# Four norm roots by reciprocal and square root, and the first weights' high parts moved to ScalarE, in a two-layer decoder step

## The chip, the cores and the metric

The kernel runs on one core of a Trainium2 chip. The metric is the device time of one execution in microseconds, the median of several runs.

## The reference

One inference step of a decoder trunk with two layers, for 512 prompt tokens and 8 x 4 sample tokens that share all weights, all in fp32. Width D is 1024. Each layer computes

```
h = rms_norm(x, gain) * (1 + scale) + shift      # shift, scale, gate g from silu(c) @ w_mod
x = x + g1 * mixer(h)                            # layer 0: forgetting attention and pooling; layer 1: native sparse attention
h = rms_norm(x, gain2) * (1 + scale2) + shift2
x = x + g2 * ((silu(h @ w_gate) * (h @ w_up)) @ w_down)

rms_norm(x, gain) = x * rsqrt(mean(x * x) + 1e-6) * gain
```

There are four norms over the model's width: before each mixer and before each SwiGLU. The mixers also norm their heads of 64; the diff does not touch these.

## The kernel before, in words

Activations lie feature by token: x is X, 8 chunks of 128 features by NT = 544 tokens (512 prompt, 32 sample), and the normed rows are H. Every large product is made of three products of parts: a matrix is split into a high part (a copy rounded to the fp32r type, WH or XH) and a low part (the value less the high part, WL or XL), and `product` (line 480) sums high x high, high x low and low x high, with 272 columns (HALF) each. The work is a sequence of stages; in each, every engine has its own program and they meet at semaphores. At the end of a stage all engines wait for each other. A `Chain` (`link`, line 77) makes an engine wait for its own last instruction.

**The norm.** ScalarE squares the chunks, VectorE sums them. TensorE multiplies the sum with a matrix of ones (`root_pe`, line 394), which gives the mean square of each token on all 128 partitions. VectorE makes V from it (line 402). ScalarE computes R = exp(-0.5 ln V) (`root_act`, lines 387 to 392) and VectorE refines R by one Newton step of three operations (`newton`, line 866). While ScalarE works, VectorE does what `root_dve` (line 399) is given as `meanwhile`. Then `norm_dve` (line 439) makes the 32 sample columns of H in three operations (lines 451 to 453), and the prompt columns chunk by chunk: H (line 462), on ScalarE XH with the shift added (`norm_act`, line 418), on VectorE XL (`low`, line 458). The H of chunk k + 1 stands before the XL of chunk k in VectorE's order. TensorE's first product of a stage waits for the weights' first cut and for the XL of chunk 0.

**The four places.** Norm 0 has its root in the setup stage (lines 237 and 305), with small index work (`small`) as `meanwhile`; the first input projection then takes the ready root. The norm before layer 1's mixer is in the input projection of `nsa_w_in`, called "in" like the first (`linear`, line 487, called at 3137). There `meanwhile` is `cut_first` (line 624): take the first half of the first 256 weight columns from RAW, cast it to WH (line 477) and subtract to WL (line 478), then let SP load the next block into that half. The norms before the SwiGLUs are in `swiglu` (line 701). Their `meanwhile` is `Seven.cut_eight` (line 969): two casts and two subtractions of 128 x 1024 (lines 972 and 973) for the first of 22 weight blocks; when they are done (`cut`, value 1) SP may load the third block into the same slot (`load`, line 912). The second block is cut by `high_eight` on ScalarE and `low_eight` on VectorE, between the first products.

**Other work around them.** In setup SP issues the loads of inputs and modulation weights, and in advance the raw weights of the first projection. In layer 0's SwiGLU TensorE also multiplies the modulation weights of layer 1 (`mod_bite`, line 330) ahead of its first product, as they land. In the two input projections side work runs between the weight blocks: the forget gate's log-sigmoid (`Forget`, ScalarE at lines 1181 to 1183: absolute value, exponential, logarithm; VectorE reads it at line 1201) and the gates of the sparse attention (`Gates`, exponential at line 1276, reciprocal at line 1287). ScalarE loads a table of functions (ACT_TABLE_LOAD) where a function isn't in the one that it holds.

Of the kernel before, what the change touches and what calls it, by code (L numbers as in the profile page):

```python
# [88 lines left out]
class Kernel:  # L89
# [297 lines left out]
    def root_act(self, act, n):  # L387
        nc, s = self.nc, n["sem"]
        act.wait_ge(s["v"], 1)
        nc.scalar.activation(n["R"], n["V"], ACT.Ln).then_inc(s["ln"], 1)  # L390
        act.wait_ge(s["ln"], 1)
        nc.scalar.activation(n["R"], n["R"], ACT.Exp, scale=-0.5).then_inc(s["r"], 1)
# [6 lines left out]
    def root_dve(self, dve, link, n, meanwhile):  # L399
        s, V = n["sem"], n["V"]  # L400
        dve.wait_ge(s["ms"], 1)
        link(self.nc.vector.tensor_scalar(V.rearrange("p (h n) -> p h n", h=2), self.ps[:, 0:2, 0:HALF], 1.0 / D, EPS, ALU.mult, ALU.add))
        dve.sem_inc(s["v"], 1)
        meanwhile()
        dve.wait_ge(s["r"], 1)
        newton(self.nc, link, n["R"], V, n["S"])

    def norm_act(self, act, n, XH, keep, meal=None, between={}):


        nc, H, s = self.nc, self.H, n["sem"]
        if n["V"] is not None:
            self.root_act(act, n)
        act.wait_ge(s["decode"], 1)
        nc.scalar.copy(XH[:, :, TP:NT], H[:, :, TP:NT]).then_inc(s["x_high"], 1)
        for k in range(KD):
            act.wait_ge(s["h"], k + 1)
            nc.scalar.activation(XH[:, k, 0:TP], H[:, k, 0:TP], ACT.Identity, bias=n["sh"][:, k, 0:1]).then_inc(s["x_high"], 1)
            if meal and k == 1 and meal[3] == KD:
                self.mod_rows(act, meal[0], meal[3] // KD - 1)  # L420
            if k in between:
                between[k]()
        for k in range(KD if keep else 0):
            act.wait_ge(s["x_cut"], k + 2)
            nc.scalar.activation(H[:, k, 0:TP], H[:, k, 0:TP], ACT.Identity, bias=n["sh"][:, k, 0:1]).then_inc(s["kept"], 1)
# [13 lines left out]
    def norm_dve(self, dve, link, n, XH, XL, cut_first, meal=None):  # L439
# [7 lines left out]
        if n["V"] is not None:  # L447
            self.root_dve(dve, link, n, cut_first)
        else:
            cut_first()  # L450
# [10 lines left out]
        for k in range(KD):  # L461
            nc.vector.scalar_tensor_tensor(H[:, k, 0:TP], X[:, k, 0:TP], A[:, k, 0:1], R[:, 0:TP], ALU.mult, ALU.mult).then_inc(s["h"], 1)
            if k == 0:
                dve.wait_ge(s["x_high"], 1)
                nc.vector.tensor_tensor(XL[:, :, TP:NT], H[:, :, TP:NT], XH[:, :, TP:NT].bitcast(F32), ALU.subtract).then_inc(s["x_cut"], 1)
            else:
                low(k - 1)
# [19 lines left out]
    def linear(self, name, w, K, blocks, x=None, out=None, residual=None, norm=None, first=None, meal=None, more=None, beside=None, squares=False, root=None, into=None, loaded=None):  # L487
# [8 lines left out]
        with self.stage() as (sb, sem):  # L496
# [12 lines left out]
            dc, x_high, x_cut, slices = sem("dc"), sem("x_high"), sem("x_cut"), sem("w_slices")  # L509
# [4 lines left out]
            with nc.Block() as block:  # L514
# [80 lines left out]
                def _(act):  # L595
                    for m in range(2):
                        act.sem_inc(pfree[m], 1)
                    if norm:
                        self.norm_act(act, n_, XH, True, meal)
# [16 lines left out]
                def _(dve):  # L616
# [7 lines left out]
                    def cut_first():  # L624
# [13 lines left out]
                        if not first:  # L638
                            dve.sem_inc(free[0], 1)

# [48 lines left out]
                    if norm:  # L689
                        self.norm_dve(dve, link, n_, XH, XL, cut_first, meal)  # L690
# [10 lines left out]
    def swiglu(self, l, meal=None, more=None):  # L701
# [3 lines left out]
        with self.stage() as (_, sem_a):  # L705
            DOWN = H[:, :, :].rearrange("p k n -> p (k n)")[:, 0:KF // 2 * 256].rearrange("p (k n) -> p k n", k=KF // 2)
            down_in = sem_a("down_in")
            with self.stage() as (sb, sem):
# [10 lines left out]
                with nc.Block() as block:  # L719
# [34 lines left out]
                    def _(act):  # L754
# [10 lines left out]
                        self.norm_act(act, n_, XH, True, meal, {2: lambda: seven.high_eight(act, 0), 5: lambda: seven.high_eight(act, 1)})  # L765
# [120 lines left out]
class Seven:  # L886
# [5 lines left out]
    def __init__(self, kernel, sem, name, WH, WL, S, E, XH, XL, TH, TL, slots):  # L892
# [4 lines left out]
        self.full = [sem(f"{name}_w_full{s}") for s in range(2)]  # L897
# [70 lines left out]

    def cut_eight(self, dve, link):
        self.raw_there(dve, 0)  # L970
        for a in range(2):
            link(self.nc.vector.tensor_copy(self.WH[:, 2 * a:2 * a + 2].rearrange("p s k n -> p s (k n)"), self.raw_parts(0, a)))
# [2320 lines left out]
```

## Time and profile before

| | before |
|---|---|
| median of 3 runs (lowest, highest) | 2348.34 us (2336.81, 2349.63) |
| profiled execution, its own time | 2347.75 us |
| its span, first to last instruction | 2346.1 us |
| mean granted TensorE clock | 0.923 |
| busy: TensorE, VectorE, ScalarE, GpSimd | 2055.0, 1356.7, 789.6, 268.6 us |

In the profile PE is TensorE (PEld its weight loads), DVE VectorE, ACT ScalarE, POOL GpSimd, SP the engine that issues most DMAs; SPq, DVEq and so on are their instruction queues. L402 is line 402 of the kernel. In a timeline each row has its start and its length in us from the start of the span, and behind the count, in brackets, how long the engine had been idle before it and what ended that. A matmul of 272 columns is one instruction; rows that follow each other closely are merged (x2), so their length is that of both with the pause between them. A table load stands under the line of the function that needs it. The granted clock is in parts of 2.4 GHz.

### The profile page before, as it was taken

The numbers are of one execution on the slowest core, as the hardware profiler recorded it, in microseconds if no ns is written. First come the engines' busy times: TensorE is split into PE (matmuls) and PEld (weight loads), VectorE is DVE, ScalarE is ACT, GpSimd is POOL, SyncE is SP. The second block draws the span as 40 slices with busy tenths as digits, with TensorE's granted clock in tenths as the row PEclk, the third lists the DMA queues.
The fourth block names the chain that finished last, engine by engine and source line by source line (L and its number), as shares of the span: only waits on it lengthen the run. The fifth ranks groups of instructions, "written<-read, shape, count | busy, mean of one in ns | idle before, by whom it ended". The sixth has DMA issues, their size and how long they took to land. (4 is left out here: it accounts for less than half of the span.)

```text
span 2346.1 us, 47705 instructions
## 1 busy us (share of the span) xinstructions
PE 2055.0 (88%) x18117; PEld 1863.6 (79%) x18117; DVE 1356.7 (58%) x2553; ACT 789.6 (34%) x1415; POOL 268.6 (11%) x430
## 2 busy tenths in 40 slices
PE   5986898879999996997699969988987687999998
PEld 3973765659999996995499969988965486999998
DVE  5336332458887634337366558777753358888732
ACT  3111331135544102013266654444521215454300
POOL 0002443000000000000012222212223100000000
PEclk8996898879999997997799989999997998999999
DMA  9348899353343221216410013434359513334321
GB/s 372 100 160 334 280 342 366 118 192 90 91 109 104 81 69 49 82 55 252 156 47 2 2 56 121 122 94 127 109 186 328 216 57 89 106 93 109 99 75 63
DMA packets 238678, 322.56 MB, mean 137 GB/s; under 512 B 18424, under 2 KB 195013, under 8 KB 231148
## 3 DMA queue, kind: packets, MB, share of 16 engines
q1 hardware_dynamic: 215317, 239.18, 31.4%
q0 software_dynamic: 21248, 77.62, 9.5%
q8 instruction: 144, 2.36, 0.4%
q10 hardware_dynamic: 1887, 2.73, 0.3%
q14 instruction: 82, 0.67, 0.1%
HBM read 311.56 MB, written 16.42 MB: 140 GB/s over the span
## 5 line engine op out<-in xcount | busy, mean ns | idle before, releaser
L2637 PE MATMUL ps<-CHi,W1H 128*128 128x256 f32 x768 | 222.2, 289 | 36.9 <-DVE CLo L2740 36.9
L2638 PE MATMUL ps<-CLo,W1H 128*128 128x256 f32 x768 | 220.3, 287 | 0.0
L2639 PE MATMUL ps<-CHi,W1L 128*128 128x256 f32 x768 | 220.1, 287 | 0.0
L957 PE MATMUL ps<-XHup,WLup 128*128 128x272 f32 x640 | 185.1, 289 | 0.0
L957 PE MATMUL ps<-XHup,WHup 128*128 128x272 f32 x640 | 183.8, 287 | 1.3 <-DVE G L1106 1.3
L957 PE MATMUL ps<-XLup,WHup 128*128 128x272 f32 x640 | 184.5, 288 | 0.0
L2637 PEld LDWEIGHTS ps<-CHi,W1H 128*128 128x128 f32 x768 | 150.5, 196 | 38.8 <-DVE CLo L2740 28.2
L2158 DVE TENSOR_REDUCE NM<-ps 128x1 f32<-128x128 f32 (+1 forms) x224 | 89.5, 402 | 124.7 <-PE ps L2037 88.4
L484 PE MATMUL ps<-XHdn,WHdn 128*128 128x272 f32 x704 | 148.3, 292 | 12.1 <-DMA Wmod<-in_w_mod 5.2
L2117 ACT ACTIVATE P<-ps,NM 128x128 f32<-128x128 f32 (+1 forms) x224 | 101.3, 458 | 160.8 <-DVE NM L2158 155.9
L2638 PEld LDWEIGHTS ps<-CLo,W1H 128*128 128x128 f32 x768 | 150.7, 196 | 0.0
L2639 PEld LDWEIGHTS ps<-CHi,W1L 128*128 128x128 f32 x768 | 150.5, 196 | 0.0
L484 PE MATMUL ps<-GL,WHdn 128*128 128x272 f32 x704 | 147.2, 291 | 0.0
L484 PE MATMUL ps<-XHdn,WLdn 128*128 128x272 f32 x704 | 146.8, 290 | 0.0
L484 PE MATMUL ps<-XHin,WHin 128*128 128x272 f32 x576 | 123.1, 296 | 21.8 <-issue 15.4
L957 PE MATMUL ps<-THup,WHup 128*128 128x272 f32 x480 | 138.0, 287 | 1.8 <-ACT Eup L1092 1.8
L957 PE MATMUL ps<-THup,WLup 128*128 128x272 f32 x480 | 138.7, 289 | 0.0
L957 PE MATMUL ps<-TLup,WHup 128*128 128x272 f32 x480 | 138.7, 289 | 0.0
L484 PEld LDWEIGHTS ps<-XHdn,WHdn 128*128 128x128 f32 x704 | 112.3, 192 | 13.0 <-issue 13.0
L957 PEld LDWEIGHTS ps<-XHup,WHup 128*128 128x128 f32 x640 | 120.6, 188 | 1.9 <-DVE G L1106 1.7
L484 PE MATMUL ps<-XHin,WLin 128*128 128x272 f32 x576 | 121.6, 293 | 0.0
L484 PE MATMUL ps<-XLin,WHin 128*128 128x272 f32 x576 | 121.3, 293 | 0.0
(564 smaller groups left out, 5338.4 us busy)
## 6 DMA issues: line engine op xcount, KB each, us to landing
H<-in_w_up SPq DMA_DIRECT2D x72, 512.0 KB, 5.1
Wearly<-in_w_mod SPq DMA_DIRECT2D x24, 1024.0 KB, 11.9
RAWdn<-in_w_down SPq DMA_DIRECT2D x14, 1408.0 KB, 6.4
RINGf<-in_cache_fox_k SPq DMA_DIRECT2D x48, 256.0 KB, 6.3
RINGf<-in_cache_fox_v SPq DMA_DIRECT2D x44, 256.0 KB, 8.2
RINGf<-in_cache_fox_v POOLq DMA_DIRECT2D x44, 256.0 KB, 6.2
RAWin<-in_nsa_w_in SPq DMA_DIRECT2D x20, 512.0 KB, 3.6
RINGf<-in_cache_fox_k POOLq DMA_DIRECT2D x38, 256.0 KB, 5.8
```

Of the source, the lines that this page charges most:

```text
L484: mm = self.nc.tensor.matmul(self.ps[:, banks + n, 0:HALF], w, x[:, n * HALF:(n + 1) * HALF], start=start, stop=stop)
L957: last = self.nc.tensor.matmul(self.ps[:, bank + b, 0:HALF], wt[:, w, k, :], x[:, k, :], start=start and k == 0 and n == 0, stop=k == 3 an ...
L2117: nc.scalar.activation(P3[:, n % 4, 0:w], ps[:, made[step] % S_BANKS, 0:w], ACT.Exp, bias=NM[:, n:n + 1]).then_inc(sems["bank_read"], 1)
L2158: nc.vector.tensor_reduce(NM[:, n:n + 1], ps[:, made[step] % S_BANKS, 0:width(*units[n])], AX.X, ALU.max, negate=True).then_inc(sems["maxi ...
L2637: nc.tensor.matmul(out, WH[:, sig, k, w], hi, start=(k == 0 and m == 0), stop=False, skip_group_check=True)
L2638: nc.tensor.matmul(out, WH[:, sig, k, w], lo, start=False, stop=False, skip_group_check=True)
L2639: last = nc.tensor.matmul(out, WL[:, sig, k, w], hi, start=False, stop=(k == KU - 1), skip_group_check=True)
```

## The change

R is now the square root of 1/V: VectorE takes the reciprocal of V into R right behind V, and ScalarE takes the square root of R in place. The Newton step stays. In the three norms inside a stage with weights the `meanwhile` is gone; in setup `small` stays, behind the reciprocal. The high part of the first weights is copied by ScalarE behind the square root (`cut_high` in `linear`, `high_start` in `Seven`), and VectorE makes the low parts inside the loop over the chunks, at k = 1, between the H of chunk 1 and the XL of chunk 0. The release of the raw weights' slot moves there too. A stage whose norm has its root ready (the first projection) cuts its weights as before.

```diff
--- before.py
+++ after.py
@@ -387,30 +387,31 @@
...
         act.wait_ge(s["v"], 1)
-        nc.scalar.activation(n["R"], n["V"], ACT.Ln).then_inc(s["ln"], 1)
-        act.wait_ge(s["ln"], 1)
-        nc.scalar.activation(n["R"], n["R"], ACT.Exp, scale=-0.5).then_inc(s["r"], 1)
+        nc.scalar.activation(n["R"], n["R"], ACT.Sqrt).then_inc(s["r"], 1)
 
...
 
-    def root_dve(self, dve, link, n, meanwhile):
+    def root_dve(self, dve, link, n, meanwhile=None):
         s, V = n["sem"], n["V"]
...
         link(self.nc.vector.tensor_scalar(V.rearrange("p (h n) -> p h n", h=2), self.ps[:, 0:2, 0:HALF], 1.0 / D, EPS, ALU.mult, ALU.add))
+        link(self.nc.vector.reciprocal(n["R"], V))
         dve.sem_inc(s["v"], 1)
-        meanwhile()
+        if meanwhile:
+            meanwhile()
         dve.wait_ge(s["r"], 1)
...
 
-    def norm_act(self, act, n, XH, keep, meal=None, between={}):
+    def norm_act(self, act, n, XH, keep, meal=None, between={}, cut_high=None):
 
...
             self.root_act(act, n)
+            cut_high(act)
         act.wait_ge(s["decode"], 1)
@@ -445,7 +446,7 @@
...
         if n["V"] is not None:
-            self.root_dve(dve, link, n, cut_first)
+            self.root_dve(dve, link, n)
         else:
@@ -464,6 +465,8 @@
...
             else:
+                if k == 1 and n["V"] is not None:
+                    cut_first()
                 low(k - 1)
@@ -506,7 +509,7 @@
...
             pfree = [sem(f"ps_free{m}") for m in range(2)]
-            dc, x_high, x_cut, slices = sem("dc"), sem("x_high"), sem("x_cut"), sem("w_slices")
+            dc, x_high, x_cut, slices, w_high = sem("dc"), sem("x_high"), sem("x_cut"), sem("w_slices"), sem("w_high")
             GROUPS = [range(a, min(a + 4, KL)) for a in range(0, KL, 4)]
@@ -593,10 +596,14 @@
...
                 def _(act):
+                    def cut_high(act):
+                        take(act, full[0], 16)
+                        nc.scalar.copy(WH[:, 0, :, :], RAW[:, 0, :, :]).then_inc(w_high, 1)
+
                     for m in range(2):
...
                     if norm:
-                        self.norm_act(act, n_, XH, True, meal)
+                        self.norm_act(act, n_, XH, True, meal, cut_high=cut_high)
                     for k in range(0 if norm or made else K):
@@ -637,6 +644,12 @@
...
                             dve.sem_inc(free[0], 1)
+
+                    def cut_first_low():
+                        dve.wait_ge(w_high, 1)
+                        link(nc.vector.tensor_tensor(WL[:, 0, :, :], RAW[:, 0, :, :], WH[:, 0, :, :].bitcast(F32), ALU.subtract))
+                        dve.sem_inc(slices, 1)
+                        dve.sem_inc(free[0], 1)
 
@@ -687,7 +700,7 @@
...
                     if norm:
-                        self.norm_dve(dve, link, n_, XH, XL, cut_first, meal)
+                        self.norm_dve(dve, link, n_, XH, XL, cut_first if n_["V"] is None else cut_first_low, meal)
                     else:
@@ -762,7 +775,8 @@
...
 
-                        self.norm_act(act, n_, XH, True, meal, {2: lambda: seven.high_eight(act, 0), 5: lambda: seven.high_eight(act, 1)})
+                        self.norm_act(act, n_, XH, True, meal, {2: lambda: seven.high_eight(act, 0), 5: lambda: seven.high_eight(act, 1)},
+                                      seven.high_start)
                         gate(0)
@@ -894,7 +908,7 @@
...
         self.slots = [x[:, 0:2048].rearrange("p (u k n) -> p u k n", u=2, k=KD) for x in slots + [H[:, 0:2048], H[:, 2048:4096]]]
-        self.full = [sem(f"{name}_w_full{s}") for s in range(2)]
+        self.full, self.started = [sem(f"{name}_w_full{s}") for s in range(2)], sem(f"{name}_w_started")
         self.high, self.cut, self.summed, self.done, self.kept, self.sums, self.used, self.x_sums, self.x_high, self.x_cut, self.dc = (
@@ -966,10 +980,14 @@
...
 
+    def high_start(self, act):
+        self.raw_there(act, 0)
+        for a in range(2):
+            self.nc.scalar.copy(self.WH[:, 2 * a:2 * a + 2].rearrange("p s k n -> p s (k n)"), self.raw_parts(0, a)).then_inc(self.started, 1)
+
     def cut_eight(self, dve, link):
-        self.raw_there(dve, 0)
         for a in range(2):
-            link(self.nc.vector.tensor_copy(self.WH[:, 2 * a:2 * a + 2].rearrange("p s k n -> p s (k n)"), self.raw_parts(0, a)))
+            dve.wait_ge(self.started, a + 1)
             link(self.nc.vector.tensor_tensor(self.WL[:, 2 * a:2 * a + 2].rearrange("p s k n -> p s (k n)"), self.raw_parts(0, a),
```

## Rows read from the trace of the kernel before

**Rows 1.** Page, part 1: busy us, share of span, instructions.

```profile
PE 2055.0 (88%) x18117; PEld 1863.6 (79%) x18117; DVE 1356.7 (58%) x2553; ACT 789.6 (34%) x1415; POOL 268.6 (11%) x430
```

**Rows 2.** Timeline, setup: start us, us, engine, line, op, [idle before <-releaser].

```profile
28.81 0.72 DVE L402 TENSOR_SCALAR V<-ps 128x544 f32<-128x544 f32 x1 [1.95 <-PE ps L396]
...
30.28 6.62 SPq L328 DMA_DIRECT2D Wearly<-in_w_mod  x4
...
32.32 0.73 DVE L868 TENSOR_TENSOR S<-Rfirst 128x544 f32<-128x544 f32 x1 [0.96 <-ACT Rfirst L392]
...
34.92 0.31 DVE L355 TENSOR_TENSOR mod<-ps,VT 128x144 f32<-128x144 f32 x1
...
37.88 0.38 SPq L1132 DMA_DIRECT2D WF<-in_ab_w_in  x1
```

**Rows 3.** Timeline, end of a projection and start of layer 1's SwiGLU.

```profile
1932.27 0.73 DVE L384 TENSOR_TENSOR H<-H 128x544 f32<-128x544 f32 x1 [0.91 <-ACT H L380]
...
1934.12 29.00 SPq L918 DMA_DIRECT2D G<-in_w_up  x8
```

**Rows 4.** Timeline, second input projection, from the root to the first products.

```profile
903.77 0.72 DVE L402 TENSOR_SCALAR PT<-ps 128x544 f32<-128x544 f32 x1 [1.52 <-PE ps L396]
...
906.59 0.66 ACT L392 ACTIVATE PT<-PT 128x544 f32<-128x544 f32 x1
...
906.71 1.22 DVE L478 TENSOR_TENSOR WLin<-RAWin,WHin 128x1024 fp32r<-128x1024 f32 x1
...
908.21 0.73 DVE L868 TENSOR_TENSOR PT<-PT 128x544 f32<-128x544 f32 x1 [0.28 <-DVE WLin L478]
...
914.23 0.74 DVE L458 SCALAR_TENSOR_TENSOR XLin<-H,mod,XHin 128x512 fp32r<-128x512 f32 x1
...
915.19 0.82 PE L484 MATMUL ps<-XHin,WHin 128*128 128x272 f32 x2 [11.46 <-issue]
```

**Rows 5.** Groups by form: line, engine, op, shapes, count | busy us, mean ns.

```profile
L1287 DVE RECIPROCAL G<-G 48x544 f32<-48x544 f32 x1 | 3.5, 3545 | 0.1
...
L392 ACT ACT_TABLE_LOAD x4 | 5.1, 1283 | 0.1
...
L980 ACT CAST WHup<-G 128x1024 fp32r<-128x1024 f32 x4 | 4.1, 1034 | 0.0
```

**Rows 6.** Timeline, first input projection, VectorE and TensorE at the second block.

```profile
61.22 0.69 DVE L477 CAST WHin<-RAWfirst 128x1024 fp32r<-128x1024 f32 x1 [5.17 <-remote]
...
63.64 0.51 PE L484 MATMUL ps<-XHin,WHin 128*128 128x272 f32 x2 [1.06 <-ACT PT L607]
```

**Rows 7.** Timeline, layer 0's SwiGLU up to its first products.

```profile
501.16 0.72 DVE L868 TENSOR_TENSOR SG<-R 128x544 f32<-128x544 f32 x1 [0.18 <-DVE WLup L973]
...
507.54 20.02 SPq L918 DMA_DIRECT2D G<-in_w_up  x4
...
513.64 1.93 PE L334 MATMUL ps<-Wlate,CV 128*32 128x512 f32 x8 [1.41 <-DMA Wlate<-in_w_mod]
...
515.51 0.82 PE L484 MATMUL ps<-XHup,WHup 128*128 128x272 f32 x2
```

**Rows 8.** Timeline, layer 1's SwiGLU from root to first low part.

```profile
1936.36 0.72 DVE L402 TENSOR_SCALAR V<-ps 128x544 f32<-128x544 f32 x1 [1.61 <-PE ps L396]
...
1944.23 0.73 DVE L868 TENSOR_TENSOR SG<-R 128x544 f32<-128x544 f32 x1 [0.18 <-DVE WLup L973]
...
1950.24 0.74 DVE L458 SCALAR_TENSOR_TENSOR XLup<-H,mod,XHup 128x512 fp32r<-128x512 f32 x1
```

**Rows 9.** Timeline, first input projection, log-sigmoid of the forget gate and its reader.

```profile
106.85 0.66 ACT L1183 ACTIVATE PT<-PT 8x544 f32<-8x544 f32 x1
...
111.86 0.71 DVE L1201 TENSOR_TENSOR PT<-PT 8x544 f32<-8x544 f32 x1 [0.28 <-DVE WLin L478]
```

**Rows 10.** Windows: length, busy us (count) by engine, PEclk, DMA share, GB/s.

```profile
926.00:931.60 5.60, 5.59 (x24) 5.59 (x25) 2.07 (x3) 1.92 (x4) 0.00 (x0) 0.50 0.64 171
...
1955.80:1962.00 6.20, 6.20 (x50) 6.20 (x50) 6.07 (x8) 5.84 (x9) 0.00 (x0) 0.99 0.01 3
```

## The prediction

> **What bounds the kernel now.** I read the busy times of the page first. TensorE is busy for 88% of the span [rows 1], so an edit pays only where TensorE stands idle and a chain of the other engines ends that idle time. The norms are such places: between the matmuls that sum the squares and the first products of the next stage TensorE has next to nothing to do. The chain that ended last holds only the output stage, so I went to the timeline around each of the four roots that the diff touches: in setup, in the second input projection ("in", layer 1) and in the two SwiGLUs. The mixers' own head norms have a logarithm and exponential of their own and are not changed.
>
> In the second projection TensorE waits 11.46 us before its first product [rows 4]. The chain is: mean square V on VectorE at 903.77, logarithm, table load and exponential on ScalarE until 907.25, VectorE meanwhile cutting the first weights until 907.93, Newton steps from 908.21, the rows of x, the first low part of x at 914.23, the product at 915.19. So the exponential was done 0.68 us before VectorE was free: the ScalarE side isn't what ends this wait, the cut is. What counts is how VectorE's own queue gets longer or shorter between V and the first low part of x.
>
> **Prices.** Each root loses one exponential and one table load (0.66 [rows 4] and 1.28 us [rows 5]) and gains one reciprocal on VectorE. The only wide one in the trace took 3.54 us on 48x544 [rows 5]. The plain operation on 8x544 took 0.71 us [rows 9] and on 128x544 0.72 us [rows 2], so the columns count and not the partitions: I take 3.54 us. Its ends are 0.72 us, were it as cheap as a plain operation, and 9.4 us, were it to grow with partitions (3.54 x 128/48). The new square root is priced as the exponential, 0.66 us; its table can load before V is there, as the logarithm's does now, and if it can't, 1.28 us come on top. Between two chained VectorE operations I take 0.2 us (0.28 us at most [rows 4]).
>
> The page "VectorE: DVE Perf Modes" of the Trainium skill (the 8-slice pipeline, "First, the fixed hardware budget") says that reciprocal is an iterative divide with a repeat count of 8. At the 0.96 GHz that the same page gives for this engine that would be an estimated 4.5 us for 544 columns, and the sum below would be 3 us higher. The row disagrees with 3.54 us, and I go by the row.
>
> **Setup.** V ends at 29.53. Before, the small index work ran beside ScalarE and was done at 31.36 (32.32 less 0.96 idle), 1.83 us after V; Newton began at 32.32 and the last VectorE operation ended at 35.23, 2.91 us later [rows 2]. After: the reciprocal runs from 29.7 to 33.3; the small work behind it ends at 35.1, longer than the square root takes (33.4 to 34.1); VectorE ends at 38.0, 2.8 us later than before. But the next stage began at 37.88, 2.65 us after VectorE was done, where another boundary takes 1.12 us (VectorE ends at 1933.00, SP starts at 1934.12) [rows 3]. SP was still issuing loads until 36.90 [rows 2], and 37.88 is 0.98 us behind that. So I read that SP opened the stage, and only 38.0 - 36.9 = 1.1 us pass on. In the projection that follows, the second block's raw weights were waited for 5.17 us and then TensorE idled 1.06 us before that block [rows 6]. The transfers issued in setup keep to their own times, so this load lands when it did, and the idle time takes up the shift. **Setup: 0.1 us** (bounds 0 and 2.8 - 1.06 = 1.7).
>
> **Second input projection.** The reciprocal runs from 904.7 to 908.2, the square root until about 909.0, so Newton begins 0.8 us later than at 908.21. The weights' high part goes to ScalarE behind the root: one 128x1024 copy of 1.03 us [rows 5], over at about 910 and needed only at 915, so nothing. Their low part (1.22 us and 0.28 us of chaining [rows 4]) is moved from a place where it hid behind ScalarE to one between the second row block and the first low part of x, and TensorE's first product waits for exactly that low part. VectorE has no idle time there that could take it. **0.8 + 1.5 = 2.3 us.** It is kept: the second half of the weights is cut when VectorE has ended the norm, and TensorE started on it only at 926 with 24 products in 5.6 us [rows 10]. The freed slot's load is issued 8 us later, and takes some microseconds of the ten that remain. If the low part were covered, 0.8 us would be left.
>
> **SwiGLU of layer 0: 0 us.** The root gets shorter here, since two casts and two low parts (4.2 us) go from in front of Newton. But before its first product TensorE has to take the last modulation weights, which landed at 513.64; the product follows at 515.51 [rows 7]. Newton began at 501.16; a root 4 us shorter and two low parts of 2.8 us put in later both end long before 513. Loads of the third weight block leave SP at 507.54 behind the modulation loads, and the slot is free by about 506. If the cover by the modulation weights were gone, it would be a gain of 1.2 us.
>
> **SwiGLU of layer 1.** V ends at 1937.08; before, the weights' cut held Newton until 1944.23 [rows 8]. After: reciprocal until 1940.8, square root until 1941.6, so Newton is 2.6 us earlier. ScalarE's two high copies (2 x 1.03 us) end near 1943.7 and aren't waited for. The two low parts, 2 x 1.22 and about 0.35 us of chaining, come before the first low part of x, which ran at 1950.24: 2.8 us. **+0.1 us**, between -2.6 (low parts covered) and +1.0.
>
> **Table loads.** The exponentials in the two projections' side work found their table there and now each needs a load of 1.28 us. The forget gate's logarithm ended at 107.51, its reader began at 111.86 [rows 9]: 4.3 us of cover. For the NSA gates I take the same, at most 1.3 us if it is not covered.
>
> **Sum.** 0.1 + 2.3 + 0 + 0.1 = 2.5 us on the profiled execution's own 2347.75 us, so 2350.3. The median of the runs is 0.6 us above that execution: **2351 us**. About 0.5%, 11.7 us, is what a measurement of this kernel can tell from no change, and the runs shown lie 12.8 us apart, so this is no change by measure.
>
> **Rivals.**
> The setup passes on in full. VectorE opened the stage after all, because the boundary of this stage takes longer than the one in rows 3. Then it is 1.7 instead of 0.1: 2352.6 us. Against it: SP's 0.98 us fits too well. Chance 0.2.
>
> The low parts are covered beside the first columns, as the change's words say. Then 0.8 us in the projection and -2.6 us in layer 1's SwiGLU: -1.7 in sum, 2346.6 us. Against it: both VectorE and the first low part of x follow each other without idle time. Chance 0.1.
>
> The reciprocal is as cheap as a plain operation. Then Newton begins 2.0 us earlier in the projection (net -0.5), 5.5 earlier in the SwiGLU (net -2.7), nothing in setup: 2345 us. The 3.54 us row speaks against it. Chance 0.05.
>
> **Slower than before:** the reciprocal is dearer on 128 partitions. It is on the path in three of the four roots (setup too, once its slack is used), so each extra microsecond costs 3; the sum passes 11.7 us where it takes 3.54 + 9.2/3 = 6.6 us or more, and at 9.4 us it would be 2368 us. The equal times of 8 and 128 partitions in plain operations speak against it. Chance 0.04. A reciprocal only 1 us dearer, 4.5 us, gives 3 us more, 2354 us, by the same mechanism; it has 0.05 of the forecast's chance and lies in its range. (The Trainium skill's repeat count, named above, is that point.)
>
> Beside these stands TensorE's clock. Products went 24 to 5.6 us at the granted clock of 0.50 (1.2 GHz) and 50 to 6.2 us at 0.99 (2.4 GHz) [rows 10]; so a microsecond at the low level costs 0.47 us. Each start after a norm begins at the low level, and the starts move. If the low stretch grows or shrinks by 3 us at three of them, that is 4 us either way. It belongs to the range and no case needs it.
>
> **How the numbers follow.** The forecast as summed has 0.57, the rivals 0.2, 0.1, 0.05, 0.04, and 0.04 is left for runs apart from the others. The range 2340 to 2358 holds the first four with the clock's 4 us, the 1.3 us of a table load in each of the projections and 1 us for the reciprocals at three places, and reaches down towards the fastest run shown (2336.81). Slower by over 0.5% is the dear reciprocal and half of what is left: 0.06; faster by as much is a low run only: 0.04; no change 0.90.
>
> **What would show it.** In the profile after: RECIPROCAL on 128x544, four times, near 3.5 us; no table load between V and the square root; setup's last VectorE operation near 38, the next stage at about 39, the second block's start still at 63 to 64. In the second projection V to first product 13.7 us instead of 11.4, with the low part of the weights directly before the first low part of x; in layer 0's SwiGLU the first product still right behind the modulation products; in layer 1's V to first low part of x still 13.9 us. I would be wrong if VectorE waited on ScalarE's high copies before a low part, or if TensorE's first product came earlier than the low part of the weights.

## The result and the profile after

The changed kernel takes 2351.99 us in the median of 20 runs (2344.60 to 2360.18), the kernel before 2344.88 us in 20 (2334.43 to 2357.62). The ratio is 1.0033, with a 95% interval from 1.0020 to 1.0046: slower by 4.7 to 10.8 us. The forecast was 2351 us, "no change" with 0.90, range 2340 to 2358. Two later executions, one of the kernel before at 2454.88 us and one of e3 at 3969.76 us, stand far apart from all others; the medians of their sets count them, and no ratio, mean or fit does. One caution first: part of that agreement is luck. The 20 runs put the kernel before 2.9 us below the execution from which the sum started (2344.88 against 2347.75), so the forecast's own +2.5 us would have given about 2347. The question of the experiments is what the rest is made of.

Part 1 of the page after, busy us (share of the span) and instructions, against [rows 1]:

```profile
PE 2058.9 (88%) x18117; PEld 1865.6 (79%) x18117; DVE 1367.2 (58%) x2552; ACT 789.9 (34%) x1414; POOL 267.3 (11%) x430
```

TensorE has the same share as before and the same products, but 3.9 us more of busy time, so part of the longer time passes while it works. The answers for lines 401 and 390 of the kernel after (duration in ns min/median/max, first and last start), against the groups of [rows 5]:

```profile
L401 DVE RECIPROCAL R<-V x2: 3552/3552/3552, 497.8 to 1944.5; 128x544 f32<-128x544 f32 x2
L401 DVE RECIPROCAL Rfirst<-V x1: 3553/3553/3553, 31.0 to 31.0; 128x544 f32<-128x544 f32 x1
L401 DVE RECIPROCAL PT<-PT x1: 3554/3554/3554, 907.1 to 907.1; 128x544 f32<-128x544 f32 x1
...
L390 ACT ACT_TABLE_LOAD  x4: 1283/1283/1283, 26.2 to 1941.4; - x4
```

The reciprocal takes 3.55 us on 128x544, as the one on 48x544 did [rows 5]: more partitions didn't make it longer. Table loads at the roots are four where eight were (line 390 and line 392 before), and in none of them does the square root wait for one.

Timeline of setup after (start us, us, engine, line, operation, [idle before <-releaser]), against [rows 2]:

```profile
30.11 7.10 SPq L328 DMA_DIRECT2D Wearly<-in_w_mod  x4
30.12 0.72 DVE L400 TENSOR_SCALAR V<-ps 128x544 f32<-128x544 f32 x1 [3.15 <-PE ps L394]
...
30.98 3.55 DVE L401 RECIPROCAL Rfirst<-V 128x544 f32<-128x544 f32 x1
...
36.48 0.72 DVE L882 TENSOR_TENSOR S<-Rfirst 128x544 f32<-128x544 f32 x1
...
39.07 0.31 DVE L355 TENSOR_TENSOR mod<-ps,VT 128x144 f32<-128x144 f32 x1
40.25 0.38 SPq L1150 DMA_DIRECT2D WF<-in_ab_w_in  x1
...
48.00 0.81 PE L487 MATMUL ps<-XHin,WHin 128*128 128x272 f32 x2 [4.50 <-issue]
```

The reader is to see three things. From the end of V, at 30.84, to the end of VectorE's last operation, at 39.38, it takes 8.54 us where it took 5.70 [rows 2]: 2.84 us more, as priced (2.8). SP was done issuing at 37.21, 2.17 us before VectorE, and the stage opened 0.87 us behind VectorE: the opener has changed. And V itself began 1.31 us later than in the execution before (30.12 against 28.81), though no instruction of VectorE or TensorE before V was changed. The stage starts at 40.25 instead of 37.88.

Timeline after, around the second block of the first projection, against [rows 6]:

```profile
61.15 0.69 DVE L480 CAST WHin<-RAWfirst 128x1024 fp32r<-128x1024 f32 x1 [2.57 <-remote]
...
62.11 0.66 PE L487 MATMUL ps<-XHin,WHin 128*128 128x272 f32 x2
...
63.70 0.41 PE L487 MATMUL ps<-XLin,WHin 128*128 128x272 f32 x2
```

The second block's cut came at 61.15, as before (61.22), because its load keeps its own time. But a pair of products still took 0.66 us at 62.11 and 0.41 us at 63.70, and the block started at 66.77 without idle time, where it was 63.64 with 1.06 us idle [rows 6]. (That row names ScalarE's copy of the sums as what ended the idle time; but after, the block started before the same copy, at 66.78, so the weights' cut is what it waited for.) The windows 60 to 64, first after, then before (us, busy us (count) of PE, PEld, DVE, ACT, POOL, PEclk, DMA share, GB/s):

```profile
60.00:64.00 4.00, 4.00 (x22) 4.00 (x21) 2.43 (x4) 0.73 (x2) 3.39 (x3) 0.57 0.61 185
```

```profile
60.00:64.00 4.00, 2.94 (x24) 2.73 (x23) 2.37 (x4) 1.23 (x2) 3.39 (x3) 1.00 0.39 116
```

Before, TensorE ran at the high level and starved (2.94 of 4 us busy); after, it was busy throughout at a mean granted clock of 0.57. This second low stretch inside the first block is not the mark of the change: it is the execution before that stands apart. The window 58 to 60 of e10 (described below), whose setup and first projection are those of the kernel before:

```profile
58.00:60.00 2.00, 2.00 (x11) 2.00 (x10) 0.00 (x0) 0.00 (x0) 1.41 (x2) 0.50 1.05 325
```

Of the fourteen profiles, eight with the old root in setup and six with the new one, only before and e1 have no such stretch of some 3 us or more. Without it the block takes 17.1 us, with it 18.4 to 18.6 us, in e7 19.8 us.

Timeline of the second projection after, against [rows 4]:

```profile
906.23 0.72 DVE L400 TENSOR_SCALAR PT<-ps 128x544 f32<-128x544 f32 x1 [1.52 <-PE ps L394]
907.09 3.55 DVE L401 RECIPROCAL PT<-PT 128x544 f32<-128x544 f32 x1
910.77 0.66 ACT L390 ACTIVATE PT<-PT 128x544 f32<-128x544 f32 x1 [5.35 <-DVEq L86]
911.33 1.03 ACT L601 CAST WHin<-RAWin 128x1024 fp32r<-128x1024 f32 x1
911.45 0.72 DVE L882 TENSOR_TENSOR PT<-PT 128x544 f32<-128x544 f32 x1 [0.81 <-ACT PT L390]
...
916.80 0.75 DVE L463 SCALAR_TENSOR_TENSOR H<-X,A,PT 128x512 f32<-128x512 f32 x1
917.47 1.22 DVE L650 TENSOR_TENSOR WLin<-RAWin,WHin 128x1024 fp32r<-128x1024 f32 x1
...
918.96 0.75 DVE L459 SCALAR_TENSOR_TENSOR XLin<-H,mod,XHin 128x512 fp32r<-128x512 f32 x1 [0.28 <-DVE WLin L650]
...
919.93 0.82 PE L487 MATMUL ps<-XHin,WHin 128*128 128x272 f32 x2 [13.74 <-issue]
```

From V to the first product it is 13.70 us (before 11.42), +2.28 where 2.3 was forecast. Newton begins at V + 5.22 (before V + 4.44: +0.78, forecast 0.8). The low part at 917.47 stands directly before the first low part of x, and the interval between those two starts is 1.49 us (forecast 1.5). ScalarE's high copy ended at 912.36, five microseconds before it was read.

Timelines of the SwiGLUs of layer 0 and layer 1 after, against [rows 7] and [rows 8]:

```profile
508.20 2.58 DVE L991 TENSOR_TENSOR WLup<-G,WHup 128x1024 fp32r<-128x1024 f32 x2
...
512.36 1.65 SPq L932 DMA_DIRECT2D G<-in_w_up  x2
...
517.58 1.93 PE L334 MATMUL ps<-Wlate,CV 128*32 128x512 f32 x8 [1.54 <-DMA Wlate<-in_w_mod]
...
519.44 0.82 PE L487 MATMUL ps<-XHup,WHup 128*128 128x272 f32 x2
```

```profile
1943.61 0.72 DVE L400 TENSOR_SCALAR V<-ps 128x544 f32<-128x544 f32 x1 [1.61 <-PE ps L394]
1944.47 3.55 DVE L401 RECIPROCAL R<-V 128x544 f32<-128x544 f32 x1
1948.14 0.66 ACT L390 ACTIVATE R<-R 128x544 f32<-128x544 f32 x1 [5.48 <-DVEq L86]
1948.71 1.98 ACT L986 CAST WHup<-G 128x1024 fp32r<-128x1024 f32 x2
1948.83 0.72 DVE L882 TENSOR_TENSOR SG<-R 128x544 f32<-128x544 f32 x1 [0.81 <-ACT R L390]
...
1954.84 2.58 DVE L991 TENSOR_TENSOR WLup<-G,WHup 128x1024 fp32r<-128x1024 f32 x2
...
1957.60 0.75 DVE L459 SCALAR_TENSOR_TENSOR XLup<-H,mod,XHup 128x512 fp32r<-128x512 f32 x1 [0.18 <-DVE WLup L991]
...
1958.50 0.79 PE L487 MATMUL ps<-XHup,WHup 128*128 128x272 f32 x2 [14.93 <-DVE XLup L459]
```

In layer 0 the first product follows the modulation products, which waited for their weights' transfer until 517.58, and VectorE's first low part of x had been ready since 511.71. The third block's load left SP at 512.36 behind those of the modulation weights, not behind VectorE. In layer 1 Newton begins at V + 5.22 (before V + 7.87), the first low part of x at V + 13.99 (before 13.88 [rows 8]).

### The profile page after: what moved, and what is told of

Read it like the earlier page. It is cut to its first block and busy times, and to the rows that moved or that the text cites. A ratio compares the mean times of both kernels' runs of the same rounds, so it can differ in the third digit from the quotient of the medians.

```text
span 2351.8 us, 47707 instructions
## 1 busy us (share of the span) xinstructions
PE 2058.9 (88%) x18117; PEld 1865.6 (79%) x18117; DVE 1367.2 (58%) x2552; ACT 789.9 (34%) x1414; POOL 267.3 (11%) x430
```

## The experiments

Each kernel is compared with the kernel before on the same chip. Local readings are from V to the first product, since V is where each root begins; before they are 11.42 us in the second projection and 14.77 us in layer 1's SwiGLU. In the other profiles with the old root and the old order they are 11.10 to 11.30 and 14.81 to 15.17 (there VectorE's cut, and Newton behind it, also waits for the weights' transfer), so differences from before alone are good to 0.3 us. As single terms of 1 to 3 us are small beside the scatter of single runs (a standard deviation of 5.1 us in the kernel before), the local readings carry most of what follows.

**The parts by themselves.** e1_setup_only: the new root in setup alone. Its core:

```
-            root = dict(V=..., R=self.root, ...)
+            root = dict(sqrt=True, V=..., R=self.root, ...)
...
+        if n["sqrt"]:
+            link(self.nc.vector.reciprocal(n["R"], V))
```

> The kernel before with the new root in setup alone. My sum (SP opens the next stage, the load of the second block takes up the rest): VectorE's last operation of setup 2.8 us later after V, next stage within 1.0 us of that, at most 1.5 us later than before; total 0.1 us slower, ratio 1.000. Rival one (VectorE opened the stage before too): next stage 2.8 us later, total 1.7 us slower. Rival two, formed on the result of the change (the idle time of 1.06 us before the second block is saved but comes back as a stretch at the low clock in the first block): 2.5 to 3 us slower, ratio 1.001, with the granted clock below 0.9 in the second half of the first block.

Measured: 1.0022 [1.0003, 1.0042], 2348.21 against 2343.33 us. VectorE ended at 38.25, SP at 37.39, and the stage opened at 39.12, 0.87 us behind VectorE and 1.24 us later than before. TensorE's idle time before the second block was 0.32 us, and that block started 0.65 us later than before (64.29). The expectation's second rival does not show here: the first block took 17.1 us, as before, at the high level throughout its second half. So the local reading is near the prediction's sum, and the 5 us of the raw medians is answered by e11 below.

e2_all_but_setup: the change in the three other norms (`sqrt=False` for the setup root, `sqrt=True` and the late cut for the rest).

> The change without its setup part. My sum: 2.3 us from the second projection and 0.1 us from layer 1's SwiGLU, 2.4 us slower, ratio 1.001; V to first product 13.7 us in the projection, V to first low part of x 14.0 us in the SwiGLU. If setup is what I undervalued, this kernel gives back some 3 to 5 us of the 7 us that the change cost; if it is a longer low clock behind the later starts, it gives back at most 1 us and the stretches at the low clock show it.

Measured: 1.0024 [1.0008, 1.0039], 2347.36 us. From V to the first product 13.70 us in the second projection, 14.90 in layer 1's SwiGLU, as expected; the raw difference is repeated in e10 below.

e3_root_only: the new root everywhere, the weights cut where they were.

```
-        nc.scalar.activation(n["R"], n["V"], ACT.Ln).then_inc(s["ln"], 1)
-        act.wait_ge(s["ln"], 1)
-        nc.scalar.activation(n["R"], n["R"], ACT.Exp, scale=-0.5).then_inc(s["r"], 1)
+        nc.scalar.activation(n["R"], n["R"], ACT.Sqrt).then_inc(s["r"], 1)
...
+        link(self.nc.vector.reciprocal(n["R"], V))
```

> The new root at all four places, the weights cut on VectorE as before (between reciprocal and Newton). Priced from rows: second projection 2.1 us (reciprocal ends 3.7 us behind V, then cast and low part 2.2 us, Newton at 910.3 instead of 908.2), layer 1's SwiGLU 1.0 us, setup 0.1 us, layer 0's SwiGLU nothing: 3.2 us slower, ratio 1.0014. A rival that blames the placement expects about nothing here.

Measured: 1.0042 [1.0024, 1.0060], 2354.44 us. The timeline of its second projection:

```profile
905.88 0.72 DVE L400 TENSOR_SCALAR PT<-ps 128x544 f32<-128x544 f32 x1 [1.52 <-PE ps L394]
...
910.58 0.69 DVE L476 CAST WHin<-RAWin 128x1024 fp32r<-128x1024 f32 x1 [0.28 <-DMA RAWin<-in_nsa_w_in]
911.41 1.22 DVE L477 TENSOR_TENSOR WLin<-RAWin,WHin 128x1024 fp32r<-128x1024 f32 x1
...
919.92 0.81 PE L483 MATMUL ps<-XHin,WHin 128*128 128x272 f32 x2 [14.07 <-issue]
```

14.04 us instead of 11.42: the reciprocal stands in front of the weights' cut, ScalarE's square root ends at 911.08 while VectorE cuts until 912.63. In layer 1's SwiGLU it is 15.93 (+1.16).

e4_place_only: the old root, the weights' high parts on ScalarE and low parts late (the reverse of e3's edit, made on the changed kernel).

> The old logarithm and exponential, the weights' high parts on ScalarE and low parts beside the first columns. Priced from rows: second projection Newton 0.9 us earlier, low part 1.5 us: 0.6 us slower; layer 1's SwiGLU Newton 4.3 us earlier, low parts 2.8 us: 1.6 us faster; the others nothing. Sum 1.0 us faster, ratio 0.9996. If the placement is what costs, this one is slower than before by more than 2 us.

Measured: 1.0006 [0.9987, 1.0025], 2345.85 us. Its second projection:

```profile
898.77 0.72 DVE L402 TENSOR_SCALAR PT<-ps 128x544 f32<-128x544 f32 x1 [1.52 <-PE ps L396]
...
902.28 0.73 DVE L883 TENSOR_TENSOR PT<-PT 128x544 f32<-128x544 f32 x1 [2.78 <-ACT PT L392]
...
908.29 1.22 DVE L651 TENSOR_TENSOR WLin<-RAWin,WHin 128x1024 fp32r<-128x1024 f32 x1
...
910.76 0.82 PE L488 MATMUL ps<-XHin,WHin 128*128 128x272 f32 x2 [12.02 <-issue]
```

11.99 us, +0.57 against before: Newton comes at V + 3.51 instead of 4.44, and 1.5 us of low part follow later. In layer 1's SwiGLU 13.17, a gain of 1.60 us. So the second half of the change costs next to nothing and gives something where two blocks were cut ahead of Newton; the reciprocal is what costs.

e5_after_again: the changed kernel, once more, in a later set.

> The changed kernel once more, beside the three variants below and the kernel before on one chip. If the cost is what the pieces show (second projection 2.3 us, SwiGLU 0.1 us, setup 1 to 3 us), it is 3.5 to 5.5 us slower at the same mean granted clock, ratio about 1.002. If the first 20 runs' 7 us are all caused by the change, then its mean granted clock is again 0.003 lower than that of the kernel before. V to first product 13.7 us in the second projection again.

Measured: 1.0038 [1.0019, 1.0057], 2356.41 against 2344.84 us; 13.70 us from V to the first product in the second projection. The mean granted clock was 0.9220 against 0.9245, lower by 0.0025: of the two outcomes named, this is nearly the second ("again 0.003 lower"). What that means is taken up behind the stages.

**A version that beats both?** e6_swiglu_place: the old root everywhere, the moved cut in the SwiGLUs alone (`late=False` for the projections).

> The kernel before, but in the two SwiGLUs ScalarE copies the high parts of the first weights behind logarithm and exponential and VectorE makes the low parts beside the first columns; setup and second projection as before. From e4: V to first product 13.2 us instead of 14.8 to 15.1 in layer 1's SwiGLU, 11.4 in the projection, nothing in layer 0's SwiGLU (still behind the modulation products): 1.8 us faster, ratio 0.9992. A rival in which TensorE's clock takes this back expects the low stretch behind the start to be longer than 4.7 us by twice the gain.

Measured: 0.9994 [0.9974, 1.0014], 2345.05 us; 13.17 us in layer 1's SwiGLU, 11.17 in the second projection. The local gain of 1.6 us is there, and the whole time doesn't tell it from nothing.

e7_pool_low: the old root and e4's placement, with the projection's low part and one of each SwiGLU's two on GpSimd.

```
+                        if norm and n_["V"] is not None:
+                            pool.wait_ge(w_high, 1)
+                            nc.gpsimd.tensor_tensor(WL[:, 0, :, :], RAW[:, 0, :, :], WH[:, 0, :, :].bitcast(F32), ALU.subtract).then_inc(slices, 1)
...
```

> As e4 (logarithm and exponential, high parts on ScalarE), but the low part of the first weights is made on GpSimd: all of it in the second projection, one of two halves in the SwiGLUs. GpSimd's 128x256 subtraction took 0.74 us, so 128x1024 is taken as 3 us, done 4 to 5 us before it is needed. Then V to first product is 10.5 us in the projection (11.4 before, 13.7 in the change) and 11.8 us in layer 1's SwiGLU (14.9 in the change): 4 us faster than before, ratio 0.998. Rival: GpSimd and VectorE hold each other up; then VectorE's Newton and x operations last longer than 0.72 to 0.75 us and the gain is gone.

Measured: 0.9998 [0.9980, 1.0016], 2344.10 us. The timeline of the Newton steps, VectorE and GpSimd:

```profile
902.12 0.73 DVE L891 SCALAR_TENSOR_TENSOR PT<-PT 128x544 f32<-128x544 f32 x1
902.23 2.82 POOL L550 TENSOR_TENSOR WLin<-RAWin,WHin 128x1024 fp32r<-128x1024 f32 x1 [405.18 <-ACT WHin L608]
902.99 2.63 DVE L892 SCALAR_TENSOR_TENSOR PT<-PT 128x544 f32<-128x544 f32 x1
```

The third Newton operation, 0.73 us elsewhere, took 2.63 us beside GpSimd's subtraction and ended 0.57 us behind it, as if it had waited for its end. Layer 1's SwiGLU repeats it (2.63 us, 0.58 us behind). The second Newton operation, which had started before GpSimd, kept its 0.73 us. From V to the first product it became 12.40 us, 0.41 more than in e4, although 1.5 us of VectorE's work were gone, and 13.73 us in layer 1's SwiGLU, 0.56 more than in e4. The page "GPSIMD Engine Reference" of the Trainium skill (Specifications, the row on the SBUF interfaces) says that VectorE's instructions with two SBUF inputs contend with GpSimd; this row agrees.

**The setup term.** e8_sp_done_early: two of SP's four modulation loads leave setup and are issued in the next stage; the root is the old one.

```
-                    for n in range(2, 6):
+                    for n in range(2, 4):
...
-                            more=lambda sp: [self.mod_load(sp, self.early, n) for n in range(6, 8)], ...
+                            more=lambda sp: [self.mod_load(sp, self.early, n) for n in range(4, 8)], ...
```

> The kernel before, with the last two of SP's modulation loads of setup issued at the start of the next stage. If SP opened that stage (36.90 us), it now opens 0.9 us behind VectorE's last operation, near 36.1 us instead of 37.9, and the first product comes 1.7 us earlier; the second block still waits for its raw weights until 61 us, so its start stays at 63 to 64 and the total is the same. If VectorE opened it before, the stage's start doesn't move. If the load of the second block isn't tied to the transfers in front of it, that start moves by 1.7 us too.

Measured: 1.0001 [0.9979, 1.0022], 2342.00 us. The timeline, setup and then the second block:

```profile
29.80 2.92 SPq L328 DMA_DIRECT2D Wearly<-in_w_mod  x2
...
34.57 0.31 DVE L355 TENSOR_TENSOR mod<-ps,VT 128x144 f32<-128x144 f32 x1
35.74 0.38 SPq L1132 DMA_DIRECT2D WF<-in_ab_w_in  x1
...
43.33 0.81 PE L484 MATMUL ps<-XHin,WHin 128*128 128x272 f32 x2 [2.14 <-issue]
...
61.01 0.69 DVE L477 CAST WHin<-RAWfirst 128x1024 fp32r<-128x1024 f32 x1 [7.12 <-remote]
...
63.44 0.51 PE L484 MATMUL ps<-XHin,WHin 128*128 128x272 f32 x2 [1.51 <-ACT PT L607]
```

SP was done at 32.72, VectorE at 34.88, and the stage opened at 35.74 instead of 37.88. So SP did open the stage before, as read. And the second block started at 63.44, almost where it was (63.64): the first block started 2.15 us earlier and took 1.5 us longer (18.6 instead of 17.1), because TensorE ran at the low level from 54.1 to 57.5 (granted clock 0.50), and the idle time behind it grew by 0.45 us, since the load kept its time (cut at 61.01).

e11_setup_only_again repeats e1, e10_all_but_setup_again repeats e2, in a later set.

> e1 once more: 1.5 to 3 us slower than before at equal mean granted clock. With e2's it gives the whole change, 4 to 5 us, if the parts add up; if they come to less, the change as a whole has a cost that neither part has.

> e2 once more: 1.5 to 2.5 us slower than before at equal mean granted clock (2.3 in the second projection, 0 in the SwiGLUs).

Measured: e11 0.9995 [0.9981, 1.0010], 2345.18 us; e10 0.9998 [0.9978, 1.0018], 2346.24 us, both against 2344.43. Neither confirms the +5 and +4 us of e1 and e2; e10's local readings are again 13.70 and 14.89.

e9_setup_thrice: e1 with two more reciprocals in setup, into a tile that Newton overwrites.

```
...
+        if n["sqrt"]:
+            for _ in range(2):
+                link(self.nc.vector.reciprocal(n["S"], V))
+            link(self.nc.vector.reciprocal(n["R"], V))
```

> e1 with two more reciprocals in setup, 7.4 us more on VectorE behind V. With the whole of SP's slack used by the first, all of them are on the path: next stage 7.4 us later than in e1, 9 us behind VectorE's old end; the first product 7.4 us later; the second block of the first projection, now far behind its raw weights, no longer waits for them and starts 10.2 - 1.7 - 1.1 = 7.5 us later than before. Total 7.5 to 9 us slower than before. If the transfers could take up more than 1.1 us, the total is below that. If a later start lowers the mean granted clock, it is clearly below 0.924 here.

Measured: 1.0038 [1.0020, 1.0056], 2354.29 against 2344.43 us. VectorE ended at 46.56 and the stage opened at 47.42, 0.86 us behind it, and setup with the first projection became 164.5 us. With the slack used up, what is added on VectorE passes on: 7.40 us more from V to VectorE's end, 8.2 us more of these two stages than in the mean of the five profiles with one. The medians differ by 9.9 us, a little above the expected 7.5 to 9. The mean granted clock is 0.9218 against 0.9242, which is the sign that the expectation named for a later start lowering it.

e12_projection_thrice: e2 with two more reciprocals in the second projection.

> e2 with two more reciprocals behind V in the second projection alone: V to first product 13.7 + 7.4 = 21.1 us, total 7.4 us slower than e2 and 9.7 us slower than before, since nothing behind that root has slack; less than 6 us over e2 if a transfer or TensorE's second start hides part of it.

Measured: 1.0046 [1.0029, 1.0063], 2356.06 us, 11.6 us above before where 9.7 were expected; mean granted clock 0.9211 against 0.9242. Its second projection:

```profile
904.22 0.73 DVE L405 TENSOR_SCALAR PT<-ps 128x544 f32<-128x544 f32 x1 [1.52 <-PE ps L399]
905.08 7.24 DVE L408 RECIPROCAL PT<-PT 128x544 f32<-128x544 f32 x2
912.46 3.55 DVE L409 RECIPROCAL PT<-PT 128x544 f32<-128x544 f32 x1
...
925.30 0.82 PE L495 MATMUL ps<-XHin,WHin 128*128 128x272 f32 x2 [21.12 <-issue]
```

21.08 us from V to the first product: the two added reciprocals and their chaining are 7.38 us (912.46 less 905.08), and it is 7.38 us more than 13.70.

**Stages in all profiles.** Each profile gives the length of each stage, here from one meeting of all engines to the next (SP's last semaphore event of line 126; the first row from the start of the span), whatever came before it. Sorted by what the kernel has in that stage (us, mean and number of profiles; in the last three rows the new root with the late cut against the old root in the old order; the tripled roots of e9 and e12 left out where they stand):

```
stage                        old root        new root        difference   forecast
setup + first projection     154.2 (8)       156.3 (5)       +2.1         +0.1
second projection            153.4 (6)       155.9 (4)       +2.5         +2.3
SwiGLU of layer 0            265.4 (5)       265.3 (5)       -0.1          0
SwiGLU of layer 1, with down 400.2 (5)       400.2 (5)        0.0         +0.1
```

The sum is +4.5 us, with a standard error of about 1.2 us from the scatter of the profiles. Single values scatter: 153.6 to 155.1 and 154.6 to 157.2 in the first row, 151.8 to 154.7 and 155.9 to 156.0 in the second. The scatter of the second row lies behind the first product: from there to the last product of the stage it is 136.3 to 139.1 us with the old root and 137.7 to 137.9 us in the four with the new one, 137.9 and 137.8 in the mean (e12, with the new root too, has 139.0). So the difference of the means is the one from V to the first product (11.25 us in the mean of the six, 13.70), the later load of the freed slot costs nothing, and against the profile of before alone the stage is only 1.3 us longer, because that one had a longer low stretch.

**What the raw ratio has beyond this.** Over all runs with a clock on record (102 of before, 32 of the changed kernel, 261 in all; the 20 of before that stand beside the first result have none) the time follows the mean granted clock of the run. A fit of the time on the kernel and that clock gives 1.48 us for each 0.001, with 2.8 us left as scatter. The runs of before have 0.9244 in the mean, those of the changed kernel 0.9215. At equal clock the changed kernel is 4.3 us slower, give or take 1.2 (95%); e1 with e11 +1.5 (1.3), e2 with e10 +0.7 (1.3), e4 -2.1 (1.7), e6 -1.4 (1.7), e7 -0.7 (1.7), e8 -0.4 (1.9), e3 +4.9 (1.9), e9 +5.8 (1.8), e12 +7.7 (1.9). The raw means differ by 8.7 us (2353.0 less 2344.3); the other 4.4 us go with the lower clock.

The figures at equal clock are too low for a change of this kind. e12 is the test: its local readings say 9.7 us, the fit 7.7. The wait behind that root passes at a granted clock of 0.50, so each microsecond added to it lowers the run's mean by itself, by (0.924 - 0.50)/2346 = 0.00018, and the fit takes 0.27 us of it away as if the run were a slow one (an estimate from these figures). With that given back, e12 comes to about 10 us and the changed kernel to 5 to 6 us, give or take 1.6, beside the 4.5 us of the stages. The two parts (1.5 and 0.7) come to less than the whole (4.3), but no further than these intervals allow.

Whether the change also lowers the clock beyond its own wait stays open, but chance alone is a poor reading. In sets on one chip the clock was lower than that of before by 0.0025 in e5, 0.0027 in e3, 0.0025 in e9 and 0.0031 in e12 (standard errors 0.0007 to 0.0011); these are the kernels with most time added. The added waits explain 0.001 of it in the changed kernel and 0.002 in e12. In the others the difference was: e1 and e11 -0.0008 and +0.0001, e2 and e10 -0.0014 and -0.0010, e4 and e6, which add nothing, -0.0018 and -0.0011 (0.0009 and 0.0007), e7 and e8 -0.0002 and +0.0001. The three stages behind the first projection alone last from 268 to 279 us in the profiles, whatever the kernel. No run here holds the clock.

## Why the prediction was right, and where it wasn't

**The class and the range held.** The interval of the ratio, 1.0020 to 1.0046, lies within the 0.5% that the text named. The number 2351 came within 1 us of 2351.99, but by a sum of 2.5 on a baseline 3 us too high; the change itself is worth 4.5 us by the stages and 7 us in the raw medians.

**The prices held.** The reciprocal: 3.54 taken, 3.55 measured. The rival of the cheap reciprocal and that of the dear one, the rival on the slower side, fell with that row, and e9 and e12 show what a dear one would have done. The Trainium skill's repeat count, on the page "VectorE: DVE Perf Modes" (the 8-slice pipeline), would have made it an estimated 4.5 us; the trace differs (3.55). The square root took 0.66 us and its table was there at every root. The forget gate now loads a table twice (at 107.92 and 109.97), and its logarithm still ended at 111.92, 3.1 us before its reader on VectorE (114.99). The gates of the sparse attention load one too (at 971.30), and their exponential ended at 973.31, 5.7 us before its reader (979.01). So both were covered; for the second the prediction had only assumed it.

**The second projection held, by its own steps.** +0.78 and +1.49 instead of 0.8 and 1.5; 13.70 us as "what would show it" said. e3 and e4 take the two apart: root alone +2.6, place alone +0.6. They don't add to 2.3, since either half alone gives up the old overlap of VectorE's cut with ScalarE's logarithm and exponential, and together they give it up only once. The rival "the low parts are covered" fell: in the changed kernel the H, the weights' low part and the first low part of x follow each other on VectorE with no more than 0.28 us between them. That it is kept over the stage was argued before and is now shown by the means of ten profiles (+2.5).

**The SwiGLUs held.** Layer 0: nothing, behind the modulation weights, in every profile. Layer 1: +0.11 up to the first low part of x, +0.1 forecast, as the difference between an earlier Newton (2.64 us) and a late low part. Its stage lost nothing either.

**The setup term failed.** The step "so only 38.0 - 36.9 = 1.1 us pass on ... and the idle time takes up the shift. Setup: 0.1 us" should have been about 2. The mechanism was right: SP opened the stage (e8), 0.98 us behind its last issue, and VectorE opens it now, 0.87 behind its last operation. Two sizes were wrong, and both for the same reason: they came from one execution.

- The slack behind SP. It was 1.67 us there (36.90 less 35.23), with V at 28.81. Over the profiles V begins between 28.3 and 30.2, with SP done between 36.0 and 37.5 (e8 apart). With the old root VectorE was done 0.5 to 1.8 us before SP in all but e8, so a late V was absorbed; with the new root VectorE is last and a late V passes on. The stage opened at 37.55 in the mean of seven profiles with the old root (e8 left out) and at 39.74 in that of five with the new one (39.12 to 40.33; e9 left out): +2.2, not +1.1.
- The idle time before the second block. Of eight profiles with the old setup only two had any (before 1.06, e8 1.51 us). In the others the first block, which began at 44.6 to 45.7, ended at 63.2 to 64.7 instead of 62.6, since TensorE fell to the low level for some 3 us inside it, so nothing was left to take a shift. The execution before is one of two profiles whose first block has no such stretch. e1 kept 0.32 us of it, the changed kernel none (its low stretch from 60 to 63.4).

The rival "the setup passes on in full" named about the right size (1.7) with the wrong cause, the boundary; its chance of 0.2 was too low. The clock's 4 us were kept for the range; the raw difference of 7 us has 2.6 us beyond the stages' 4.5, and whether those are the clock's is not shown. The low stretch in the first block is no piece of the change's cost, as most profiles of either root have it.

**What came of the change's aim.** The exponential and its table load (1.94 us) that it removes were hidden behind VectorE's own work and its wait for the weights in three of the four norms and stood out by 0.96 us in setup [rows 2]; the reciprocal that replaces them was hidden only by the transfers in layer 0's SwiGLU and, for a part, by SP's issues in setup.

## What to carry to other kernels

Before a step of a waiting engine is replaced by one on the engine that others wait for, ask which of the two was hidden: 2 us of ScalarE behind a weight cut were free, 3.55 us of reciprocal on VectorE were not, and the moved weight cut alone (e4, e6) was the better half of the change. A slack or an idle time of a microsecond read from one execution is a sample: look at what sets both of its ends, and if one of them moves from run to run, price the step at its mean over several profiles, or carry it in the range in full. And where a run's time follows the granted clock, look at the clock before a few microseconds are put down to the edit, but don't take the figure at equal clock for the cost: a wait that passes at the low level lowers the mean clock itself, and a run with a known added wait (here e12) tells how much of it the comparison takes away.

## What the runs showed of the hardware

- The reciprocal takes 3.552 to 3.554 us for 544 columns on 128 partitions and 3.545 us on 48, about 6.5 ns a column at this width, five times the 0.72 us of a plain operation of the same size.
- At the end of setup the next stage opened 0.98 to 0.99 us behind SP's last issue where SP was last, and 0.86 to 0.87 us behind VectorE's last operation where that was last.
- A VectorE operation of 0.73 us took 2.63 us while GpSimd subtracted one 128x1024 tile from another, and ended 0.57 us behind it (e7, at two places).
- In twelve of fourteen profiles TensorE, busy throughout, ran at the low level for some 3 us or more in the later part of the first projection's first block; the block took 18.4 to 19.8 us with that and 17.1 us without.
- In the waits behind the norm roots TensorE stands at a granted clock of 0.50 (905 to 915 us before, 905 to 925 us in e12).
- 0.001 of mean granted clock goes with 1.48 us of this kernel's time: the runs of before scatter by 5.1 us (standard deviation), and 2.8 us are left over all kernels once kernel and clock are taken out.
